# The number of filler matmuls around two of the token transposes, in a two-block float32 model on one core

## The reference, cut to what matters

```python
def first_block(x, mem, ...):
    for i in range(2):
        z = x @ (w_in_a if i == 0 else w_in_b)      # i=0: SGU mixer, i=1: short convolution
        xa = memory_cross_attention(q, mem, w_kv[i])
        o = concatenate([tok, xa], -1) @ w_out[i]
        x = layer_norm(ALPHA * x + o, ln1_g[i], ln1_b[i])
        f = grouped_moe(x, ...)                     # 16 experts, top 2 of one group of 4
        x = layer_norm(ALPHA * x + f, ln2_g[i], ln2_b[i])
    return x

def second_block(x, ...):
    for l in range(2):
        h = rmsnorm(x, norm_g[l])
        p = h @ w_in[l]                             # latents, gates, q, k, v of three branches
        ...                                         # latent attention, forgetting attention, RWKV-7 scan
        merged = sigmoid(g_a)*(o_a@w_pa) + sigmoid(g_b)*(o_b@w_pb) + sigmoid(g_c)*(o_c@w_pc)
        x = x + merged @ w_out[l]
    return x
```

## Time and profile before

| | |
|---|---|
| median of three runs | 1604.57 us (1600.95 to 1605.22) |
| profiled execution, its own time | 1605.22 us |
| its span, first to last instruction | 1603.4 us |
| TensorE matmuls (PE) busy | 1524.7 us, 95% |
| VectorE (DVE) busy | 789.8 us, 49% |
| ScalarE (ACT) busy | 540.2 us, 34% |
| granted TensorE clock, mean | 0.985 of full |
| memory traffic | 340.28 MB, mean 212 GB/s |
| chain that ended last | PE 83%, DVE 11%, ACT 2%, issue 2%, DMA 1% |

### The profile page before, as it was taken

How to read it: one execution, slowest core, us unless ns; L and a number is a source line. 1 busy time by engine, 2 the same in 40 slices (tenths; PEclk the granted TensorE clock), 3 DMA queues, 4 the chain that set the end, 5 groups by cost and what they waited for, 6 DMA issues and landing times.

```text
span 1603.4 us, 20977 instructions
## 1 busy us (share of the span) xinstructions
PE 1524.7 (95%) x8914; PEld 1060.3 (66%) x8914; DVE 789.8 (49%) x1144; ACT 540.2 (34%) x835; POOL 25.4 (2%) x35
## 2 busy tenths in 40 slices
PE   6999999998999999998999999999999999999998
PEld 6856544445945444446877676987688776669875
DVE  4724112125524121227676664774467766557743
ACT  4512111103302101014653755442246537354421
POOL 0000000000000000000000000100000000001000
PEclk9999999999999999999999899999999999999999
DMA  8449999992459999983433335002444323240031
GB/s 353 170 185 413 421 422 423 422 421 113 170 228 384 421 423 422 422 366 110 171 115 110 116 122 183 1 1 105 142 169 158 132 92 135 98 162 1 2 110 74
DMA packets 47477, 340.28 MB, mean 212 GB/s; under 512 B 5296, under 2 KB 5296, under 8 KB 7568
## 3 DMA queue, kind: packets, MB, share of 16 engines
q1 hardware_dynamic: 45504, 328.03, 51.8%
q0 software_dynamic: 1872, 10.80, 1.7%
HBM read 337.76 MB, written 1.05 MB: 211 GB/s over the span
## 4 chain that ended last, share of the span: by engine, by line
PE 83%; DVE 11%; ACT 2%; issue 2%; DMA 1%; DVEq 0%; SPq 0%; ACTq 0%
PE bank L505 52%; PE bank L796 14%; PE bank L837 7%; PE bank L740 4%; PE bank L508 3%; DVE d_lo L1651 2%; PE bank L769 1%; PE bank L774 1%; ACT arena L1249 1%; DVE arena L1628 1%; DMA ring<-wsecond 1%; ACT d_hi L1286 0%; PE bank L822 0%; DVE xT_lo L1635 0%; DMA ring<-wfirst 0%
## 5 line engine op out<-in xcount | busy, mean ns | idle before, releaser
L1651 DVE TENSOR_TENSOR d_lo<-ring,d_hi 128x2048 fp32r<-128x2048 f32 (+2 forms) x96 | 215.4, 2250 | 150.2 <-ACT d_hi L1286 150.1
L505 PE MATMUL bank<-arena 128*128 128x128 f32 (+10 forms) x2016 | 229.5, 286 | 23.6 <-ACT arena L1249 10.3
L1286 ACT ACTIVATE d_hi<-ring 128x2048 fp32r<-128x2048 f32 (+2 forms) x96 | 180.1, 1880 | 154.8 <-PE bank L505 85.9
L505 PEld LDWEIGHTS bank<-arena 128*128 128x128 f32 (+6 forms) x2016 | 196.1, 179 | 50.3 <-issue 24.3
L1249 ACT ACTIVATE arena<-bank 128x512 f32<-128x512 f32 (+3 forms) x222 | 125.3, 582 | 278.9 <-PE bank L505 183.7
L505 PE MATMUL bank<-xT_hi,d_hi 128*128 128x256 f32 x592 | 167.2, 282 | 4.1 <-DVE d_lo L1651 2.1
L505 PE MATMUL bank<-xT_hi,d_lo 128*128 128x256 f32 x592 | 166.1, 281 | 0.0
L505 PE MATMUL bank<-xT_lo,d_hi 128*128 128x256 f32 x592 | 165.5, 280 | 0.0
L505 PE MATMUL bank<-ring,arena 128*128 128x512 f32 (+2 forms) x384 | 158.7, 571 | 5.7 <-ACT arena L1527 3.5
L505 PE MATMUL bank<-d_hi,xT_hi 128*128 128x512 f32 (+1 forms) x400 | 160.8, 402 | 1.0 <-DVE xT_lo L1635 0.7
L505 PE MATMUL bank<-d_hi,xT_lo 128*128 128x512 f32 (+1 forms) x400 | 157.1, 393 | 0.0
(11 more groups left out here) (308 smaller groups left out, 1767.7 us busy)
## 6 DMA issues: line engine op xcount, KB each, us to landing
ring<-wmoe SPq DMA_DIRECT2D x84, 1024.0 KB, 13.6
ring<-wsecond SPq DMA_DIRECT2D x80, 1024.0 KB, 4.6
arena<-wmoe SPq DMA_DIRECT2D x72, 1024.0 KB, 12.5
ring<-wfirst SPq DMA_DIRECT2D x30, 1024.0 KB, 4.7
wide<-wmoe SPq DMA_DIRECT2D x24, 1024.0 KB, 13.3
xT_raw<-wmoe SPq DMA_DIRECT2D x12, 1024.0 KB, 11.9
rows<-lnrows POOLq DMA_DIRECT2D x4, 1024.0 KB, 9.5
ring<-wsecond SPq DMA_DIRECT2D x4, 848.0 KB, 9.9
```

Of the source, the lines that this page charges most:

```text
L505: mark(nc.tensor.matmul(o, lhsT, rhs, start=start, stop=stop, skip_group_check=loose), full)
L1286: nc.scalar.activation(d_hi[h % NHIGH][:, 0:width], raw[u % NRAW][:, 0:width], ACT.Copy).then_inc(sem("piece_high"), 1)
L1651: v.tensor_tensor(d_lo[u % NRAW][:, 0:width], raw[u % NRAW][:, 0:width], d_hi[h % NHIGH][:, 0:width], SUB).then_inc(sem("piece_low"), 1)
```

## The change

Two calls of `transpose_tokens` get other numbers of fillers.

```diff
@@ L632: place A, layer 1 of the first block @@
-                    transpose_tokens(x_nat, "x_first", "x_ready", 0, 3, 2)
+                    transpose_tokens(x_nat, "x_first", "x_ready", 4, 2, 2)
@@ L982: place B, layer 0 of the second block @@
-                transpose_tokens(y_nat, "h_first", "h_ready2", (6, 5)[l], 0, (2, 6)[l])
+                transpose_tokens(y_nat, "h_first", "h_ready2", (13, 5)[l], 0, (2, 6)[l])
```

## The result

The changed kernel takes 1613.58 us in the median of ten runs (1606.74 to 1618.88), beside 1604.99 us of before (ten runs, 1600.83 to 1606.59). It is slower by 8.6 us between these medians, where 5.6 were forecast, and lies just above the range of 1606.0 to 1613.5. The ratio, which goes by 27 runs of the changed kernel and not by these ten, is 1.0063, with a 95% interval of 1.0045 to 1.0082; that is 7 to 13 us. The profiled execution took 1609.85 us, with a span of 1608.0, 4.6 us above the span of before.

A forecast was written before the change was run, and what follows sets the result against it. TensorE was taken to bound the kernel, with 83% of the chain that ended last. Place A +0.9 and place B +4.7 gave +5.6 us on 1604.57, so 1610.2 us, range 1606.0 to 1613.5.

The forecast's parts named there:

- Slower: Whole kernel: outcome slower by more than about 0.3% (4.8 us), chance 0.62.
- B: Transposes of h (call at L982): six fillers ahead become thirteen, delaying TensorE by +4.7 us, bounds +3.1 to +6.1.
- A: Transposes of x (call at L632): fillers 0/3/2 become 4/2/2, costing +0.9 us, bounds -0.7 to +2.2.
- What lies behind B: From 741.62 us on: TensorE leads, weight loads move with it, nothing swallows the delay, no further change.
- the distance named in the prediction: First projection matmul behind place B to span's end: stays 861.8 us; a change over 2 us means wrong.
- The swallowed delay: Behind either place: a wait for VectorE, ScalarE or a load absorbs the delay; 1605 to 1606 us, chance 0.10.
- The cheap filler: Place B: thirteen fillers fit the cover at 0.58 us each at most; about 1605 us, chance 0.01.
- The faster case by the clock: Two later 10 us low-clock stretches keep full clock, giving back about 11 us: 1599.2 us, chance 0.07.

The follow-up runs named there:

- 6 full, 7 tiny: Kernel before with seven tiny fillers (8 rows by 8 columns) added behind the six full ones at place B; ratio 1.0024.
- B alone: Kernel before with only place B changed, six fillers to thirteen; ratio 1.0047.
- second set: The changed kernel run again unaltered, against the kernel before; median 1612.59 us, ratio 1.0046.
- the third: The changed kernel run once more unaltered, on the chip of its version with eight tiny fillers, against the kernel before; median 1615.12 us, ratio 1.0067.
- A alone: Kernel before with only place A changed, fillers 0/3/2 to 4/2/2; ratio 0.9999.
- A 0/1/2: Kernel before with one filler instead of three between the tiles at place A; ratio 1.0008.
- thirteen full and eight tiny fillers: Kernel before with thirteen full fillers and eight tiny ones behind them at place B, place A as before; ratio 1.0045.

## Why the prediction was wrong

**Direction and places: right.** Slower was the likeliest case, with 0.62, and the two places cost what was worked out. B was to cost +4.7 and the profile has +5.01. The 0.33 between them is a gain that I had counted and that did not come: the sixteen transposes without their wait between the tiles take 0.39 us less, but VectorE's subtractions start 1.3 us behind the first transpose and take 2.48 us as before, and the two last fillers, which now end sooner, no longer cover them.

**A: the mechanism right, the size short.** +0.9 was forecast, as a size with two values of the clock behind it. The five profiles with 4/2/2 have +0.78, +0.68, +0.62, +0.77 and once +2.25, where the clock stayed low under nearly all of the four fillers. I had measured it against one profile of before, though, and that one sat at the dear end. Among the profiles that leave A as it was, two have it 1.2 us (no fillers at B) and 1.54 us (6 full, 7 tiny) cheaper than the first profile, because the clock was low for 3.4 us and not 6.8. The mean of those six is -0.55 and of the five with the change +1.02, so A costs about 1.6 us and not 0.9. The step that failed here is the price of the kernel before, taken from one execution.

**What lies behind B: wrong, and this is the step that failed.** The prediction said "So the loads move with TensorE and nothing swallows the delay", and asked that the distance from B's first projection to the end stay within 2 us. The loads do start with TensorE. But one of them landed 1.0 us later than it should, at the one point where the chain goes through a load. Nothing in the order of TensorE's work says this. What moved was the place in the work where the next 16 KB of instructions are fetched, by 11 us, from behind the wait that TensorE has until 783.85 to ahead of it. I had counted the added fillers as time only and not as program length. The experiment with seven tiny fillers has the length without the time, and the load is late there too; eight tiny ones more move the fetch out again, and the load is back at 4.7 to 4.9 us. In the three profiles of the change the step is +1.21, +1.80 and +1.40, mean 1.5. The load's part of it is 1.0, 1.7 and 1.2 us. The rest is low clock over what follows, 1.4 to 1.5 us, less the 1.3 us of slack at 806.

In the profile after, the distance named in the prediction came out at 1608.0 - 746.1 = 861.9 against 861.8: that sign was met by luck, since the step of +1.2 was cancelled by low stretches that fell shorter later. In the second and third profiles of the change the distance is 1610.8 - 745.6 = 865.2 and 1610.5 - 745.6 = 864.9, over 3 us more, and there the sign says that the prediction is wrong. A sum over 860 us was too coarse a test for a microsecond.

**The sum.** A 1.6, B 4.9 and the step 1.5 are 8.0 us, beside 8.6 between the medians. A and the step hold low clock, so I also asked what the runs give at equal clock. The low-clock time of a run is 2 x (1 - mean clock) x span. It was 46 us in the mean over the 89 runs of before listed with their clock, and 51, 50 and 54 us in the three sets of the change. Within a kernel a run is about 0.37 us longer for each us of it (a straight line through the runs of each, with about 0.9 us of scatter). At 46 us the lines give 1604.2 for before and 1612.0, 1611.4 and 1610.7 for the three sets: +6.5 to +7.8 us. The seven fillers at B alone stand at +4.9 there. What is above that in the runs (+7.5 us in the second set, +10.6 in the third) goes with more low-clock time. How much of that belongs to the change, and whether the later place of the work brings it, stays open. The load's microsecond doesn't stand out in these lines either: six full and seven tiny fillers stand at -0.2 us.

**The rivals.** The swallowed delay didn't come: B's 5.0 us are there at 775 in full. The cheap filler, with the 131 ns of the page "TensorE: Matmul & The Clock Gate" of the Trainium skill, didn't either: 26 records in 13.12 us are 1.0 us a filler with the low stretch in it. The faster case by the clock was not met, but what it lives from is real. The stretch of 10 us behind 889 was low in the profile after as well, and the other one (1320 us) was not. It wasn't either in the profiles of A alone, of A 0/1/2 and of thirteen full and eight tiny fillers, and the one behind 889 wasn't in that of B alone. Each time that was worth 3.9 us, beside the 5.5 that I had. It comes with and without fillers ahead, so it looks like chance from one execution to the next and not like the edit's doing; that isn't tested further.

## What to carry to other kernels

A filler is free only up to the point where what stands behind it must start: read that distance and divide by the price of one (0.86 us). Look past the first wait, since here it was 0.72 us to the first tile, but 1.2 us with the wait for the second, and one more filler was free. Added instructions are program length as well as time. Where the critical chain goes through a DMA load, look at where the instruction fetches fall before and after the edit, since one of them in that load cost 0.9 to 1.7 us here. And where the granted clock has two states, a price taken from one profile may be that of one state: take a second profile of the kernel before, too.

## What the runs showed of the hardware that I had not expected

A single fetch of 16 KB of instructions, 1 packet among 144, goes with a 1 MB load that takes 5.6 to 6.5 us (five profiles) instead of 4.5 to 4.9 (eight), and moving the fetch by tiny instructions moves the load between the two. Fourteen tiny matmul records (8 columns of weights, 8 moving columns) behind twelve full ones lengthened the run from 6.95 to 7.35 us, 0.03 us each. Executions of the kernel before on one chip differ by up to 12 us (1600.53 to 1612.33), and most of that goes with their low-clock time. Where it falls differs too: two profiles with the same code at place A had them for 3.4 and for 6.8 us there.
